# Second block's modulation computed during two projections instead of during the latent attention, with the latent sets spread, the half norms' partition sums moved up and the rotated tile kept free of a unit

## The reference

```python
# every layer of the first block
shift, scale, gate = _modulation(c, ada_w[i], ada_b[i])
h = _rmsnorm(x, norm_g[i]) * (1.0 + scale) + shift
y = _diff_attention(...) if i == 0 else _mla(...)
x = x + gate * y

# _mla: 8 heads, latents of 384 (queries) and 256 (keys, values), a rotated part of 64 columns
proj = h @ w_in
q_a, c_kv, k_pe, z = jnp.split(proj, ...)
q = (_rmsnorm(q_a, q_a_norm_g) @ w_q_b)       # per head 128 plain and 64 rotated columns
kv = (_rmsnorm(c_kv, kv_a_norm_g) @ w_kv_b)   # per head 128 of k and 128 of v
p = softmax((q_nope k_nope^T + q_pe k_pe^T) * scale)
o = (p @ v) * silu(z);  y = o @ w_out

# second block: 6 * 1024 columns of modulation, used from its first norm on
mod = (silu(c_2) @ w_ada_2 + b_ada_2)
shift1, scale1, gate1, shift2, scale2, gate2 = jnp.split(mod, 6)
```

## Time and profile before

| | us |
|---|---|
| median of 3 runs (3041.2 to 3047.51) | 3043.05 |
| the profiled execution | 3049.86 |
| its span in the trace | 3048.1 |
| TensorE busy in the span | 2791.4 (92%) |
| VectorE busy | 1687.0 (55%) |
| ACT busy | 1317.0 (43%) |

### The profile page before, as it was taken

One profiled execution on the slowest core, in us unless ns is written; L12 is line 12 of the kernel. 1 busy time (PEld: TensorE's weight loads), 2 busy tenths in 40 slices (PEclk: granted clock), 3 DMA queues, 4 the chain that ended last, 5 costly groups with the idle time before them and its releaser, 6 DMA issues.

```text
span 3048.1 us, 35097 instructions
## 1 busy us (share of the span) xinstructions
PE 2791.4 (92%) x13113; PEld 2182.2 (72%) x13113; DVE 1687.0 (55%) x2236; ACT 1317.0 (43%) x1878; POOL 0.2 (0%) x4
## 2 busy tenths in 40 slices
PE   7999999996889898898988889988799999999997
PEld 4777777774778676666766667666577878878775
DVE  7678888886453155555555535554664434334344
ACT  5666666663233233333333435655334323123232
POOL 0000000000000000000000000000000000000000
PEclk9999999997999999999999899999799999999998
DMA  7211111101211111211212210000211111111111
GB/s 262 89 49 34 48 48 43 34 28 55 97 38 43 48 51 48 71 47 50 68 56 82 80 43 28 22 15 15 97 35 48 43 47 46 50 48 41 49 38 72
DMA packets 216082, 168.08 MB, mean 55 GB/s; under 512 B 9562, under 2 KB 203058, under 8 KB 215986
## 3 DMA queue, kind: packets, MB, share of 16 engines
q1 hardware_dynamic: 215504, 166.61, 17.5%
q10 hardware_dynamic: 482, 0.18, 0.0%
HBM read 153.66 MB, written 13.11 MB: 55 GB/s over the span
## 4 chain that ended last, share of the span: by engine, by line
PE 79%; DVE 8%; ACT 6%; DVEq 3%; issue 2%; DMA 2%; SPq 0%; ACTq 0%
PE PS L509 18%; PE PS L511 18%; PE PS L510 18%; PE PS L1223 4%; PE PS L1887 3%; PE PS L1196 2%; PE PS L1210 2%; PE PS L1842 1%; PE PS L1200 1%; PE PS L1877 1%; PE PS L2351 1%; PE PS L2364 1%; DVEq L2029 1%; PE PS L2375 1%; DVE rest L500 1%
## 5 line engine op out<-in xcount | busy, mean ns | idle before, releaser
L509 PE MATMUL PS<-h_high,w_high 128*128 128x512 f32 x2096 | 842.9, 402 | 68.5 <-DVE h_low L943 23.7
L510 PE MATMUL PS<-h_low,w_high 128*128 128x512 f32 x2096 | 827.2, 395 | 0.0
L511 PE MATMUL PS<-h_high,w_low 128*128 128x512 f32 x2096 | 826.6, 394 | 0.0
L509 PEld LDWEIGHTS PS<-h_high,w_high 128*128 128x128 f32 x2096 | 400.2, 191 | 167.9 <-issue 56.2
L511 PEld LDWEIGHTS PS<-h_high,w_low 128*128 128x128 f32 x2096 | 399.8, 191 | 86.3
L510 PEld LDWEIGHTS PS<-h_low,w_high 128*128 128x128 f32 x2096 | 400.2, 191 | 81.1 <-issue 1.4
L531 DVE TENSOR_TENSOR w_low<-raw_weights,w_high 128x1024 fp32r<-128x1024 f32 (+2 forms) x156 | 179.5, 1153 | 217.4 <-ACT w_high L526 216.7
L526 ACT ACTIVATE w_high<-raw_weights 128x1024 fp32r<-128x1024 f32 (+2 forms) x156 | 155.8, 1000 | 235.2 <-PE PS L511 223.9
L1300 ACT ACTIVATE residual<-PS,rest 128x1024 f32<-128x1024 f32 x128 | 141.5, 1111 | 178.9 <-DVE rest L1430 178.9
L2907 DVE SCALAR_TENSOR_TENSOR gated<-rest,gated 128x1024 f32<-128x1024 f32 x44 | 56.6, 1285 | 253.7 <-ACT gated L2875 253.7
L801 DVE SCALAR_TENSOR_TENSOR residual<-PS,rest,residual 128x512 f32 (+1 forms) x106 | 78.6, 750 | 196.6 <-PE PS L511 190.5
(11 more groups left out here) (336 smaller groups left out, 4115.4 us busy)
## 6 DMA issues: line engine op xcount, KB each, us to landing
raw_weights<-in_w_in SPq DMA_DIRECT2D x59, 512.0 KB, 4.0
activations<-in_w_ada SPq DMA_DIRECT2D x16, 1536.0 KB, 7.0
raw_weights<-in_w_up SPq DMA_DIRECT2D x44, 512.0 KB, 3.8
raw_weights<-in_w_out SPq DMA_DIRECT2D x24, 512.0 KB, 4.2
rest<-in_ada_w SPq DMA_DIRECT2D x16, 576.0 KB, 4.9
activations<-in_ada_w SPq DMA_DIRECT2D x8, 1024.0 KB, 14.0
x_kept<-residual SPq DMA_DIRECT2D x2, 4096.0 KB, 12.4
residual<-x_kept SPq DMA_DIRECT2D x2, 4096.0 KB, 13.0
```

The costliest lines, as they stand in the source:

```text
L509: e.matmul(out_, wh[:, k, :], xh[:, k, cols], start=first, stop=False)
L510: e.matmul(out_, wh[:, k, :], xl[:, k, cols], start=False, stop=False)
L511: return e.matmul(out_, wl[:, k, :], xh[:, k, cols], start=False, stop=last_k)
```

## The change

- **Units.** `mod_products`, `load_mod` and `pe_mod` of the latent attention go. Units 0 to 6 are done in out0 (`units=True`), one a tile: after TensorE's tile u comes unit u's small matmuls, after VectorE's tile u comes `mix_out` of unit u and the products of unit u+1. Units 7 to 15 are done in `latent_input`, one a tile, except at the rotated tile (index 5), which has none. Their stage buffers are three places of 3 x 1024 columns: A in the scratch area, B and C in the gate area; units 10 to 15 all use C. SP loads them between the weight tiles, and waits for the products of the unit that had the buffer. The products of a unit are not cut into parts any more.
- **Input projection.** The unit's matmuls use bank 4, so tiles rotate through two pairs of banks (2 * (i % 2)), not three; ACT waits for the products of units 9 and 15 before it writes the gate tiles that lie in B and C. The second buffer pair of the first two tiles (`next_split`) moves down by 1024 columns.
- **Latent sets.** `BEFORE` and `AFTER` are new (below), Q1 waits for Q0's readers in place of a unit.
- **Half norms.** In the plain norms `stat_pe` of the second half comes after the first k in place of the fourth; in the fused norm before the k loop, and ACT's `rstd` after tile 0, `second_rstd` after tile 3, VectorE's `middle` after tile 2.

```diff
-    def mod_products(e, m, c_at, ks=range(NT)):
+    mix_stage = [view(at, NT, MCH) for at in (sc_at + 2 * S, g_at, g_at + 5 * S)]
+    mix_ld = in_ld[9:12]
+    def mix_load(e, u, i):
+        e.dma_start(mix_stage[i], w_cols("w_ada_2", MCH * u, MCH)).then_inc(mix_ld[i], 16)
+    def mix_products(e, u, i, arrived):
+        e.wait_ge(mix_ld[i], arrived)
+        e.wait_ge(s["md_pe"], u + (MIX_M + 1))
+        x = mix_stage[i]
+        last = e.tensor_scalar(macc, x[:, 0, :], silu_c[:, 8:9], None, ALU.mult)
+        for k in range(1, NT):
+            e.drain()
+            last = e.scalar_tensor_tensor(macc, x[:, k, :], silu_c[:, 8 + k:9 + k], macc, ALU.mult, ALU.add)
+        last.then_inc(s["md_acc"], 1)
+    def mix_out(e, u):
+        mod_out(e, u + MIX_M, 48 + 3 * u, column["b_ada_2"] + 3 * u, 4)
...
# OutProj.sync
+            if self.units:
+                for sm, v in self.src_ready:
+                    wait(e, sm, v)
+                mix_load(e, 0, MIX_A)
+                e.wait_ge(self.gl, self.bg + self.kt)
+                mix_load(e, 1, MIX_B)
...
+                    if self.units:
+                        e.wait_ge(s["md_acc"], 2 * it + (MIX_M + 1 + j))
+                        mix_load(e, 2 * it + (2 + j), (MIX_A, MIX_B)[j])
# OutProj.tensor
                 self.tile_pe(e, 0, 0, True)
+                self.unit_pe(e, 0)
                 self.tile_pe(e, 1, 1)
+                self.unit_pe(e, 1)
# OutProj.vector
+            if self.units:
+                mix_products(e, 0, MIX_A, 32)
...
                     self.tile_dve(e, 2 * it + j, j, True)
+                    if self.units:
+                        mix_out(e, 2 * it + j)
+                        mix_products(e, 2 * it + (j + 1), (MIX_B, MIX_A)[j], 16 * it + (32 + 16 * j))
# NormHalves.scalar and vector
-                if t == 3:
+                if t == (0 if self.fused else 3):
                     self.rstd(e, 1)
-                if t == 5 and self.fused:
+                if t == 3 and self.fused:
                     self.second_rstd(e, 1)
-                if t == 4 and self.fused:
+                if t == 2 and self.fused:
                     self.middle(e, 1)
# pe_two_tiles
+        if halves.fused:
+            halves.stat_pe(e, 1)
...
-                if h == 0 and k == 3:
+                if h == 0 and k == 0 and not halves.fused:
                     halves.stat_pe(e, 1)
# latent_input
+        UNITS = [(8, 4), (9, 5)] + [(10, 6)] + [(u, u - 2) for u in range(11, 16)]
+                for u, at in UNITS:
+                    if at == i:
+                        e.wait_ge(s["md_acc"], MIX_M + u - (1 if u < 11 else 0))
+                        mix_load(e, u, unit_at(u))
-                if i == KP + 3:
+                if i == KP + 2:
                     e.wait_ge(kd, 2)
                 else:
-                    wait(e, ev, i - 2 if i < KP + 3 else i - 3)
+                    wait(e, ev, i - 1 if i < KP + 2 else i - 2)
+                if 2 <= i <= KP or KP + 2 <= i <= KP + 6:
+                    mod_pe(e, MIX_M + 5 + i - (i > KP), 4)
+                if i == KP + 1:
+                    e.wait_ge(s["md_acc"], MIX_M + 10)
+                if i == KP + 6:
+                    e.wait_ge(s["md_acc"], MIX_M + 16)
+                u = i + 6 - (i > KP)
+                if 2 <= i <= KP or KP + 2 <= i <= KP + 6:
+                    mix_out(e, u - 1)
+                if 1 <= i < KP or KP + 1 <= i <= KP + 5:
+                    mix_products(e, u, unit_at(u), 32 + 16 * unit_count(u))
# latent_attention
-        BEFORE = {1: "V1", 3: "Q0", 5: "K0"}
-        AFTER = {0: "V0", 1: "R0", 2: "R1", 4: "Q1", 5: "K1"}
+        BEFORE = {0: "V0", 1: "R0", 2: "R1", 4: "Q1", 5: "K0", 6: "K1"}
+        AFTER = {0: "V1", 3: "Q0"}
```

More of the change, by code:

```diff
@@ L485, in scalar_tables @@
         exp_and_log(e)
-    def mod_products(e, m, c_at, ks=range(NT)):
[L491 to L502, removed]
+    MIX_A, MIX_B, MIX_C = 0, 1, 2
+    mix_stage = [view(at, NT, MCH) for at in (sc_at + 2 * S, g_at, g_at + 5 * S)]
+    mix_ld = in_ld[9:12]
+    MIX_M = 12
+    def mix_load(e, u, i):
[11 more added lines that the diff above has]
+        mod_out(e, u + MIX_M, 48 + 3 * u, column["b_ada_2"] + 3 * u, 4)
     def mm3(e, out_, w, k, x, cols, first, last_k):
@@ L735, in tensor, with unit_pe @@
                 self.last_pe(e)
+        def unit_pe(self, e, u):
+            if self.units:
+                mod_pe(e, u + MIX_M, 4)
         def last_pe(self, e):
@@ L833, in vector @@
                     self.tile_dve(e, 2 * it + j, j, True)
+                    if self.units:
+                        mix_out(e, 2 * it + j)
+                        mix_products(e, 2 * it + (j + 1), (MIX_B, MIX_A)[j], 16 * it + (32 + 16 * j))
             self.tile_dve(e, 6, 0, False)
+            if self.units:
+                mix_out(e, 6)
             if self.halves is None:
@@ L1637, in tensor @@
                 e.wait_ge(s["ws_low"], base + i + 1)
-                if i == KP + 3:
+                if i == KP + 2:
                     e.wait_ge(kd, 2)
                 else:
-                    wait(e, ev, i - 2 if i < KP + 3 else i - 3)
+                    wait(e, ev, i - 1 if i < KP + 2 else i - 2)
                 for h in range(2):
                     for k in range(NT):
-                        last = mm3(e, banks(2 * (i % 3) + h), split[i % 2], k, H2, slice(h * HALF, (h + 1) * HALF),
+                        last = mm3(e, banks(2 * (i % 2) + h), split[i % 2], k, H2, slice(h * HALF, (h + 1) * HALF),
                                    k == 0, k == NT - 1)
@@ L1778, in load_weights @@
                                 w_cols("w_q_b", (P + ROPE_W) * n.h + ((P + ROPE_W) * j + P), ROPE_W)).then_inc(wqr_ld, 16)
-        def load_mod(e, m):
-            e.dma_start(stage, w_cols("w_ada_2", MCH * m, MCH)).then_inc(in_ld[9], 16)
         def sync(e):
@@ L1792, in head @@
                 load_weights(e, t.next())
-                for n in range(2):
-                    e.wait_ge(s["md_acc"], 2 * t.h + 13 + n)
-                    load_mod(e, 2 * t.h + 1 + n)
             head(Head(0, 0, 0))
@@ L1907, in pe_head @@
                     pe_set(e, t, BEFORE[q])
-                if q == 7:
-                    pe_mod(e, t, 1, more)
                 pe_trans(e, t, q)
@@ L1912, in pe_head @@
                     pe_set(e, t, AFTER[q])
-                if q == 3:
-                    pe_mod(e, t, 0, more)
         def tensor(e):
@@ L2083, in vector @@
             dve_head(e, Head(7, 3, 1), Head(6, 3, 0), False)
-            dve_mod_out(e, Head(7, 3, 1), 1)
             dve_gate(e, Head(7, 3, 1), 1)
@@ L2983, in _build @@
     diff = diff_attention()
-    out0 = OutProj("w_out0", 0, NT, 16, True, [], [(diff["pj"], 64)], [diff["gated"]], 16, H2)
+    out0 = OutProj("w_out0", 0, NT, 16, True, [], [(diff["pj"], 64)], [diff["gated"]], 16, H2, units=True)
     norm1 = NormHalves(out0, 6, gain_col, shift_col(24))
```

45 lines of the change are left out of this document (13 added, 32 removed).

## The result

The changed kernel takes 3017.7 us (median of 4 executions, 3014.57 to 3018.76) where the kernel before took 3042.12 beside it: ratio 0.9915, 95% interval 0.9899 to 0.9930. The forecast was 3006 us, a gain of 36.8; the medians give 24.4 and 33.3, the two profiled executions (spans 3048.1 and 3017.0) 31.1.

A forecast was written before the change was run, and what follows sets the result against it. TensorE was taken to bound the kernel, VectorE costing only where TensorE waits for it. Attention -38.1, units +15.0 and norms -13.7 sum to -36.8 us, from the median of 3043.05 to about 3006 us; range 2985 to 3022.

The forecast's parts named there:

- The sum: Whole kernel: attention -38.1, units +15.0 and norms -13.7 give -36.8 us, to about 3006 us.
- Part 1: Latent attention: sets respread, fewer TensorE waits and less slow clock; with the units' leaving -38.1 us, 32.6 in six heads.
- part 2: Modulation units moved from the attention to the output and input projections, where they cost +15.0 us.
- rival 2: Attention: the waits move; it gains only its 16 units (9.4) and a little clock (4): 3031 us, chance 0.10.
- the matmul group: Projections: a unit's 3 small matmuls take TensorE 0.59 us, +4.1 us in the output and +5.3 in the input projection.
- The single stage buffer: Input projection: units from 10 on share one buffer; TensorE is held for the last four, +5 us (0.5 to 10).
- Rivals 3 and 5: Input projection: 3, units wait for late loads, up to 3060 us, 0.04; 5, tiles wait for bank pairs, 3039 us, 0.04.
- Part 3: Three norms: partition sums moved up end VectorE's waits of 4.42, 6.59 and 4.87 us almost wholly, -13.7 us.
- Rivals 1 and 2: Rival 1, attention: TensorE nearly fed, clock up, gains 45 + 6 instead of 38, 2989 us, chance 0.15; for 2 see rival 2.
- Head 7: Last attention head: gains its two units, gives nearly all back at the PV product behind V1; 0.5 us gained.

The follow-up runs named there:

- c2: The changed kernel with the latent sets placed as before, the units still in the two projections: 3013.42 us, ratio 0.9879 to the kernel before.
- e1: The kernel before with one multiply of each unit in place of eight, a probe with wrong results: 3020.2 us, ratio 0.9911.
- d1: The kernel before without the 16 units (loads, products, matmuls and additions left out), a probe: 3008.61 us, ratio 0.9879.
- d2: The changed kernel without the 16 units in the two projections, a probe: 2998.57 us, ratio 0.9845 to the kernel before.
- c4: The changed kernel with a fourth stage buffer for units in the input projection: 3012.63 us, ratio 0.9884 to the kernel before.
- c3: The changed kernel with the partition sums of the half norms back where they were: 3029.77 us, ratio 0.9937 to the kernel before.
- c1: The changed kernel itself, run again in another job: 3016.59 us against 3049.9 for the kernel before, ratio 0.9896.

## Why the prediction was right, and where it was not

**The sum.** -36.8 forecast; -31.1 in the traces, -33.3 in the larger comparison, -24.4 in the first. The range of 2985 to 3022 held the time. Of the 12 us between 3006 and 3017.7 some 6 lie in the terms and 6 in taking the difference over to a median of before that came out low.

**Part 1 and the first part of part 2, attention: right number, wrong cause.** The forecast priced the units' leaving at 12 x 0.59 us and gave all other gain, some 25 us of waits and clock in six heads, to the new places of the sets. The runs show the reverse. With the units gone and the sets left where they were (c2) the six heads take 351.5 us; with the units gone and the sets spread 351.1; with the sets as before and one multiply a unit (e1) 364.0. The step that failed is the assignment of the waits in the earlier trace rows: the 8.6 us at the transposes, some 4 to 5 of K1's 13.5 (9.3 in e1, 8.4 in c2) and most of the slow clock belonged to the chained multiplies in VectorE's queue. The remark under rival 2, "VectorE is busy 53% there and loses 5 us of products with each unit", had this fact in hand and used it only against the rival. Of the listed waits of K1, the forecast was right that the spread ends them; but without products they were down to 1.41 us, and the new order puts 2.3 us at the transposes of tile 3 in odd heads (forecast 2.5, found three times: 6.9 us) and 0.6 at scores and PV products in their place. Total of new waits: 17.4 forecast, 16.9 found. That the stage came out at 34.9 us for 32.6 is luck in this sense: the forecast counted every wait of the stage as lost and so did not need to know which edit ended it. Put to the units alone the same terms gave 13 us, and d1 gave 37.8.

**Part 2, units in the projections.** +15.0 forecast; 15.5 by d2, +16.9 by the stretches (+0.7 at tile 2 counted with the first norm). The term that was mis-sized is the matmul group. In the output projection it costs 0.9 us, not 0.59: two additions of neighbouring tiles in the changed kernel,

```profile
807.43 1.41 DVE L819 SCALAR_TENSOR_TENSOR residual<-PS,rest,residual 128x512 f32 x2
...
819.21 1.41 DVE L819 SCALAR_TENSOR_TENSOR residual<-PS,rest,residual 128x512 f32 x2
```

stand 11.78 us apart where the earlier trace rows have 10.88. In the input projection it costs 0.7: tiles of c4, without waits, are 11.6 us long. The 0.59 was read from one start to the next in the attention; the products around the group are stretched too. The single stage buffer was right in size by a partly wrong count: +5 forecast as waits at four units, 5.1 measured as 2.8 of waits at three units, 1.7 of slow clock and 0.6 of other stretching. Its periods were 12.4 to 13.4 us against a tile of 11.6, where 13.5 against 11.5 was forecast. Nothing else appeared: VectorE's slack in the output projection was enough (one wait of 0.15 us), and the two pairs of banks cost only the wait ahead of tile 2 (2.49 us against 1.81, 0.7 where 0.6 was forecast). Rivals 3 and 5 are out.

**Part 3, norms.** 13.7 forecast, 13.2 by c3, 12.3 in the traces. Right, with its mechanism.

**Rivals 1 and 2.** Neither came: the six heads won 34.9 us, between the 45 of the first and what the second left. The second had one thing right that the forecast had not, that moving the sets mostly moves the waits: 21.1 us of them in c2 and 16.9 in the changed kernel, with TensorE busy 330.9 and 334.2 us, make the same stretch within 0.4 us. It had the wrong price for the units.

**Head 7** gave back 0.9 us where 0.5 of gain was expected: d1, without its units, takes the same 42.6 us from fourth PV product to fourth PV product as before, so the units cost nothing there. The 0.9 us belong to the new order, which has 43.5 in all seven of its traces.

## What to carry to other kernels

When a filler task leaves a stage, price it by its whole footprint: the matmuls, and every instruction that an in-order queue holds behind its pieces. A wait in the profile is booked to the instruction that released it; look at what stood ahead of that one in its own queue, and at the chain of the stage, before crediting a reorder of the consumer's side. A wait can also cost more than its length, by the clock of what comes behind it (2.8 us of waits, 5.1 in all, in c4). A change made of several edits can hit its forecast stage by stage and still be explained wrongly; putting one edit back tells it apart for the price of a run, and the c2 run here says that the reordered sets could have been left alone.

## What was not expected of the hardware

A group of three small matmuls between two runs of 512-column products costs a tile 0.9 us in the output projection, although the next product starts 0.69 us behind the group's start; in the changed kernel:

```profile
819.29 0.83 PE L1046 MATMUL PS<-rest 128*128 128x1 f32 x6
819.98 0.48 PE L510 MATMUL PS<-h_high,w_high 128*128 128x512 f32 x1
820.30 0.40 PE L511 MATMUL PS<-h_low,w_high 128*128 128x512 f32 x1
```

From the last product ahead of the group (819.02) to the second one behind it 1.28 us pass, where two ordinary steps take 0.46: 0.82 us, most of the 0.9. In the input projection the same group costs 0.7 (0.58 us to the next product); why less stays open. And 84 multiplies less on VectorE (seven of each of the 12 units in six heads, 50 us of work on an engine half idle) moved TensorE's end by 22 us: 386.0 us against 364.0 in e1, of which some 8 are the granted clock rising from 0.97 to 0.99 (an estimate: 0.02 of 386). In one and the same order of instructions a pair of heads takes 115.9 or 117.6 us: 117.6, 117.5 and 115.9 in the changed kernel, 117.6, 115.9 and 115.9 in c1; the granted clock of the long ones is 0.99, of the short ones 1.00.
